# Four modulation sums moved to the first query stage, and wider rows of gates in DRAM

## The chip, the cores and the metric

The kernel runs on one core of one Trainium2 chip. The metric is device time in microseconds (us). Lower is better. Everything is computed in float32. Where the text says "parts", a float32 number has been cut into a high and a low part whose products are added up.

## The reference, cut to what matters

Two transformer blocks follow one another. The second block has two layers, and each layer ends in a PEER feed-forward: every token picks 16 of 16384 experts for each of 8 heads, and sums the experts' outputs by gate weights. Each layer has six modulation vectors, which are products of a condition with a 1024 x 6144 matrix.

```python
for i in range(DEPTH_2):                      # two layers, 0 and 1
    mod_x = jnp.split((silu_c @ ada_w[i] + ada_b[i])[:, None, :], 6, axis=-1)
    mod_c = jnp.split(silu_cc @ ada_w[i] + ada_b[i], 6, axis=-1)
    hx = modulate_2(x, norm_mix[i], mod_x[0], mod_x[1])
    hc = modulate_2(ctx, norm_mix[i], mod_c[0], mod_c[1])
    ...                                       # attention of layer i
    x = x + mod_x[2] * yx
    hx = modulate_2(x, norm_ffn[i], mod_x[3], mod_x[4])
    if last:
        x = x + mod_x[5] * peer(hx, peer_w_q[i], peer_keys[i], peer_u[i], peer_v[i])
    else:
        ...                                   # the 256 context tokens too
        y = peer(jnp.concatenate([hc, hx], axis=1), peer_w_q[i], ...)

def peer(h, w_q, sub_keys, u_tab, v_tab):
    q = (t @ w_q).reshape(b * n, PEER_HEADS, 2, PEER_KEY_DIM)
    s = jnp.einsum('thcd,hcnd->thcn', q, sub_keys)      # then top-k: expert, gate
    act = jax.nn.gelu(jnp.einsum('td,thkd->thk', tb, jnp.take(u_tab, eb, axis=0)))
    return jnp.einsum('thk,thkd->td', gb * act, jnp.take(v_tab, eb, axis=0))
```

## The kernel before

**Stages and queues.** The kernel is a list of stages. Each engine runs the stages in order, by its own program. A stage's first instruction on an engine waits (`enter`) until the stage before it has raised `stage_done`. SyncE (SP) issues, in one order written out by hand, the loads of the weights into a ring of four slots of 1 MB (`ring<-in_weights`, line 3576), and among them the other loads and stores of the PEER stages. ScalarE (ACT) and GpSimd (POOL) issue DMAs of their own.

**The PEER feed-forward of layer index 0** works on 512 tokens. Its stages are these:

- `Norm`.
- `PeerQuery` makes the queries: 8 chunks of weights, each cut into parts by ACT (L280) and VectorE (DVE, L286), with 48 matmuls of 512 columns per chunk on TensorE (PE; L319 for the first two chunks, L2310 for the other six). At its start ACT stores the 2 MB of `xT` in DRAM (`x_kept<-xT`, L2322).
- `PeerScores`.
- `PeerHidden` walks over 64 pairs of expert rows. 384 tokens are done densely, as if each token used all experts. The other 128 tokens ("gathered") fetch their own rows by indirect DMA (L2500, dot products L2534). From pair 33 on it also makes the dense matrix of gates, eight tokens (a "lot") at a time, two lots for a pair: DVE makes one-hot rows (L3054 to L3059), PE multiplies them (L2955), and ACT copies the result into one of two blocks in SBUF (L2864). A block holds 32 tokens, so four lots. It is stored to DRAM in four pieces of 512 KB (`gates<-arena`, L2776), one after each of the next lots, and ACT may write over a block only when its pieces of two blocks before have landed. Activations are also stored, for each pair (L2759).
- `PeerValues` walks over the 64 pairs again. SP loads gates (L3210) and activations (L3214), DVE multiplies them (L3293) and makes low parts (L3297, L3300), ACT makes high parts (L3271), and PE does 48 matmuls of 384 columns per pair (L3377). Beside this POOL gathers the rows of values (L3115) for the 128 other tokens into five buffers, and DVE adds them (L3132), two for a pair. `first_loads` fetches the first two groups of gates near the end of `PeerHidden`.

Layer index 1 has the same stages for 256 tokens.

**Side modulation.** The modulation vectors are not made on PE. POOL loads tiles of 512 KB of the modulation matrix (`arena<-in_side_weights`, L557) into four buffers in turn, each when the step that read the buffer before is done. DVE multiplies each tile by a column of the condition and adds it to a running sum: 8 tiles to a sum, the first by L574, the others by L577. This is done in groups, beside a stage that has room. Before, the fourth and last group (`SECOND`) makes all of layer index 1's vectors beside `PeerValues` of layer index 0: eight sums (vectors 0 and 1 under two conditions, 2 to 5 under one), 48 tiles and 64 steps, one step for each pair. PE later turns the sums into columns (`SideTurn`): vectors 0 and 1 in the `Norm` that follows, vectors 2 to 5 (`second_rest`) after the attention of layer index 1.

**The gates in DRAM** are laid out per partition as (group of expert rows, block of 32 tokens, rows of the group x 32 tokens). A group has 4 rows, so the run that one block writes is 4 x 32 x 4 bytes = 512 bytes. A load of a group's gates is one piece of 12 x 512 bytes for each partition.

The lines that set the layout and the order of loads are these:

```python
GATE_ROWS = (4, 4)
...
sp.dma_start(self.gates[:, groups, b, :],
             self.block[:, b % 2, rows, :].rearrange("column (group row) t -> column group (row t)", row=each))
...
def vector(self, dve):                       # PeerQuery
    self.k.enter(dve, self.s)
    each_chunk(dve, 8, lambda c, r, i: self.w.low(dve, c, r))
```

In `PeerQuery` the low parts of chunks 0 and 1 are made ahead, in the `Norm` before it, and `low` skips them. There are two buffers for parts, so chunk 2's high part is made when PE has finished chunk 0.

Of the kernel before, what the change touches and what calls it, by code (L numbers as in the profile page):

```python
# [8 lines left out]
F32 = mybir.dt.float32  # L9
# [38 lines left out]
GATE_BLOCK = (32, 32)  # L48
GATE_ROWS = (4, 4)

# [53 lines left out]
class Signal:  # L104


    def __init__(self, sem, base):
        self.sem, self.base = sem, base
# [17 lines left out]
class Core:  # L126


    def __init__(self, nc, ctx, io):
# [375 lines left out]
class SideModulation:  # L505


    FIRST_BLOCK, MLA_FIRST, MLA_LATER, SECOND = range(4)

    def __init__(self, k):  # L510
# [4 lines left out]
        own = [k.hT[:, 4 * i:4 * i + 4, 0:SEQ] for i in range(2)]  # L515
        self.buffers = [wide(22528, 4), wide(22528, 4), wide(4096, 2) + wide(14336, 2), wide(19456, 4)]
        self.sums = [wide(26624, 4) + context + [lru], context + wide(26624, 4),
                     wide(24576, 6), own + context[1:] + wide(25600, 5)]
# [6 lines left out]
        self.steps = k.count_of("side_steps", sum(DT * len(c) for g in self.groups for _, _, c in g))  # L525
        self.work, self.totals = [], []
        n_tiles, n_steps = 0, 0
        for g, group in enumerate(self.groups):
            work, totals = [], []
            for layer, m, conds in group:  # L530
                mine = list(range(len(totals), len(totals) + len(conds)))
                totals += [[layer, m, cond, 0] for cond in conds]
                for t in range(DT):
                    ops = []
                    for total, cond in zip(mine, conds):
                        n_steps += 1
                        ops.append((total, cond, t, totals[total][3], n_steps))
                        totals[total][3] = n_steps
                    work.append((n_tiles, ops))
                    n_tiles += 1  # L540
            self.work.append(work)
            self.totals.append(totals)
# [7 lines left out]
    def loads(self, pool, g):  # L550


        buffers = self.buffers[g]
        for i, (n, _) in enumerate(self.work[g]):
            if i >= 4:
                pool.wait_ge(self.steps.sem, self.steps.at(self.work[g][i - 4][1][-1][4]))
            pool.dma_start(self.like(buffers[i % 4], buffers[i % 4]), self.k.io["side_weights"][n])\  # L557
                .then_inc(self.loaded[i % 4].sem, 16)
            yield

    def like(self, flat, other):
        return flat if len(other.shape) == 2 else flat.rearrange("p (a b) -> p a b", b=SEQ)

    def begin(self, dve, g):

        def steps():
            for i, (n, ops) in enumerate(self.work[g]):
                w = self.buffers[g][i % 4]
# [11 lines left out]

        self.todo, self.total = steps(), sum(len(ops) for _, ops in self.work[g])
        self.done = 0
# [29 lines left out]
class SideTurn:  # L612
# [10 lines left out]
    def tensor(self, pe):  # L623
        side, k = self.side, self.side.k
        for n, i in enumerate(self.which):
            pe.wait_ge(side.steps.sem, side.steps.at(side.totals[self.g][i][3]))
            total = side.sums[self.g][i]
            for q in range(DT):
# [1015 lines left out]
class TokenProduct(Stage):  # L1644
# [6 lines left out]

    def __init__(self, k, name, n_k, tiles, lhs, out, at=None, norm=None, steps={}, norm_rows={}, chain=None):
        self.norm, self.steps, self.norm_rows = norm, steps, norm_rows
        self.chain = chain or (norm and norm.chain)
# [5 lines left out]
        self.act_copied = k.count_of("rows_act_copied", self.even[-1])  # L1660
        self.dve_copied = k.count_of("rows_dve_copied", self.odd[-1])

    def wait_bank(self, pe):
# [587 lines left out]
def diff_stages(k, normed, second_rest):  # L2251
# [13 lines left out]
                            10: ([("roots", 1)], [("scale", 1)]), 11: ([], [("rotate", 1)])},  # L2265
                     norm_rows={0: 1, 1: 3}),
    ]
# [18 lines left out]
class PeerQuery(Stage):  # L2286

    def __init__(self, k, l, T, h, queries):  # L2290
        self.k, self.s, self.T, self.h, self.q = k, k.stage(), T, h, queries
# [42 lines left out]
    def vector(self, dve):  # L2334
        self.k.enter(dve, self.s)
        each_chunk(dve, 8, lambda c, r, i: self.w.low(dve, c, r))
        self.finish(dve, (self.copied, 8), *([(self.kept, 16)] if self.kept else []))


class PeerScores(Stage):  # L2340

    def __init__(self, k, l, n, high, queries, scores):
        self.k, self.s, self.g, self.n, self.q, self.scores = k, k.stage(), FIRST[f"peer{l}_keys"], n, queries, scores
        self.products = k.count_of("peer_scores", n)
        self.copied = k.count_of("peer_scores_copied", n)
# [835 lines left out]
class PeerValues(PeerTable):  # L3183
# [61 lines left out]
    def sync(self, sp, load):  # L3245
# [13 lines left out]

        walk(sp, 0, self.pairs, 4, body)  # L3260

# [66 lines left out]
    def gpsimd(self, pool):  # L3328
# [4 lines left out]
        if self.side:  # L3333
            work, loads = self.side.work[self.side.SECOND], self.side.loads(pool, self.side.SECOND)
            ends = np.cumsum([len(ops) for _, ops in work]).tolist()
            issued = 0
# [107 lines left out]
def peer_stages(k, l, side=None, gate=None):  # L3444
# [6 lines left out]
    scores = k.room(work, T // P, 2 * PEER_HEADS, P)  # L3451
    before = [Norm(k, [p[:4] for p in parts], high, after=gate), PeerQuery(k, l, T, (high, k.hT_split[:, :, 0:T]), queries),
              PeerScores(k, l, T // P, high, queries, scores)]
    hidden = PeerHidden(k, l, T - (SPREAD if l else GATHERED), scores, work)
# [38 lines left out]
def program(nc, io):  # L3493

    with ExitStack() as ctx:
# [20 lines left out]
        peer_gate = turn(2, (5,), 7)  # L3516
        second_gain = turn(3, (0, 1), 1, layer=(1, 0))
        second_rest = turn(3, (2, 3, 4, 5), 7, layer=(1, 1), column=SEQ)
        lru = Recurrence(k)
# [224 lines left out]
```

## Time and profile before

| | us |
|---|---|
| median of three runs | 3320.55 |
| lowest, highest | 3320.46, 3329.16 |
| the profiled execution, its own time | 3321.39 |
| its span, first to last instruction | 3319.5 |
| around the span | 1.89 |
| TensorE's mean granted clock | 0.983 |

Times in the profile count from the start of the span. Engine "busy" is time in instructions, "PEclk" is the clock that TensorE was granted (1.00 is 2.4 GHz, 0.50 is 1.2 GHz), and the DMA share is the mean busy share of the core's 16 DMA engines. For layer index 0, `PeerQuery` runs from 1033 to 1124 us, `PeerHidden` from 1141 to 1741, and `PeerValues` from 1741.6 to 2274.4. The part of `PeerHidden` in which gates are made is about 1420 to 1676.

### The profile page before, as it was taken

What the parts mean: (1) busy time and instruction counts of PE and PEld (TensorE: products, weight loads), DVE (VectorE), ACT (ScalarE), POOL (GpSimd) and SP (SyncE); (2) the same over time, 40 slices, a digit from 0 to 9 for tenths busy, and PEclk for the clock granted to TensorE, in tenths of its full rate; (3) what the DMA queues carried; (4) which work ended last, traced back from release to release, by engine and by line L of the source; (5) the groups of instructions that cost most, each with busy time, mean ns of one, the idle gap of its engine ahead of it and who ended that gap; (6) DMA issues with size and microseconds to landing.
All of it is one profiled execution on the core that took longest, in us unless ns stands there. A gap on an engine that the chain in (4) does not pass through costs nothing.

```text
span 3319.5 us, 52879 instructions
## 1 busy us (share of the span) xinstructions
PE 3176.7 (96%) x20142; PEld 2920.0 (88%) x20142; DVE 2481.6 (75%) x4079; ACT 1466.8 (44%) x1864; POOL 1063.9 (32%) x706
## 2 busy tenths in 40 slices
PE   7999889999999999999999999999988999999999
PEld 5998689856777899999999999998868898989998
DVE  6877568686764479878849999897665797757777
ACT  5434444322443333366633333334234567874443
POOL 0110000010000278877763335551000698721110
PEclk9999899999999999999999999999998999999999
DMA  8984157461012267799999999994203578999996
GB/s 321 333 307 171 47 190 251 160 228 61 4 39 102 94 228 273 267 323 384 380 393 393 379 377 411 409 409 175 93 1 120 183 237 300 386 370 333 351 350 231
DMA packets 305610, 835.27 MB, mean 252 GB/s; under 512 B 22432, under 2 KB 185504, under 8 KB 254368
## 3 DMA queue, kind: packets, MB, share of 16 engines
q1 hardware_dynamic: 180096, 534.82, 44.3%
q0 software_dynamic: 67968, 247.49, 19.3%
q10 hardware_dynamic: 57376, 50.72, 4.5%
q8 instruction: 104, 1.70, 0.2%
q14 instruction: 66, 0.54, 0.0%
HBM read 750.10 MB, written 82.84 MB: 251 GB/s over the span
## 4 chain that ended last, share of the span: by engine, by line
PE 82%; DVE 5%; DMA 5%; ACT 3%; POOL 2%; issue 1%; SPq 1%; another core or an unknown queue 0%; ACTq 0%; DVEq 0%; POOLq 0%
PE ps L3377 16%; PE ps L2936 11%; PE ps L862 7%; PE ps L3360 6%; PE ps L2912 5%; PE ps L1688 5%; PE ps L873 4%; PE ps L3362 3%; PE ps L2310 3%; DMA gates<-arena 3%; PE ps L2914 3%; PE ps L319 3%; PE ps L1430 2%; PE ps L1412 2%; POOL arena_split L2886 2%; PE ps L2150 2%
## 5 line engine op out<-in xcount | busy, mean ns | idle before, releaser
L2886 POOL TENSOR_TENSOR arena_split<-ring,arena_split 128x1024 fp32r<-128x1024 f32 x228 | 570.9, 2515 | 900.6 <-ACT arena_split L2804 898.3
L2936 PE MATMUL ps<-xT_split,arena_split 128*128 128x384 f32 x2048 | 534.0, 337 | 3.1 <-ACT xT L2834 2.6
L3377 PE MATMUL ps<-arena_split 128*128 128x384 f32 x3072 | 532.7, 334 | 2.3 <-DVE arena_split L3300 2.3
L3377 PEld LDWEIGHTS ps<-arena_split 128*128 128x128 f32 x3072 | 532.5, 188 | 2.6 <-issue 2.6
L286 DVE TENSOR_TENSOR arena_split<-ring,arena_split 128x2048 fp32r<-128x2048 f32 x128 | 292.9, 2291 | 245.1 <-ACT arena_split L280 244.3
L3271 ACT ACTIVATE arena_split<-ring 128x2048 fp32r<-128x2048 f32 x126 | 241.7, 1918 | 492.1 <-PE ps L3377 306.6
L280 ACT ACTIVATE arena_split<-ring 128x2048 fp32r<-128x2048 f32 x128 | 244.4, 1915 | 376.9 <-PE ps L862 133.3
L2936 PEld LDWEIGHTS ps<-xT_split,arena_split 128*128 128x128 f32 x2048 | 371.8, 188 | 4.2 <-issue 4.2
L3297 DVE TENSOR_TENSOR arena_split<-ring,arena_split 128x2048 fp32r<-128x2048 f32 x128 | 293.2, 2291 | 94.8 <-ACT arena_split L3271 86.6
L2912 PE MATMUL ps<-hT_split,arena_split 128*128 128x448 f32 x1024 | 338.7, 379 | 6.9 <-POOL arena_split L2886 3.9
L557 POOL DMA_DIRECT2D arena<-in_side_weights x152 | 82.8, 546 | 817.5 <-DVE arena L577 285.0
L2936 PE MATMUL ps<-hT_split,arena_split 128*128 128x384 f32 x1024 | 342.9, 335 | 0.0
L3360 PE MATMUL ps<-arena_split 128*128 128x448 f32 x1024 | 327.2, 379 | 0.8 <-DVE arena_split L3300 0.8
L2914 PE MATMUL ps<-hT_split,arena_split 128*128 128x224 f32 x1024 | 273.7, 267 | 0.0
L2804 ACT ACTIVATE arena_split<-ring 128x1024 fp32r<-128x1024 f32 x256 | 268.9, 1053 | 8.4 <-DMA ring<-in_weights 8.4
L3362 PE MATMUL ps<-arena_split 128*128 128x224 f32 x1024 | 271.0, 265 | 0.0
L3115 POOL DMA_INDIRECT arena<-in_weights,arena x128 | 214.9, 1679 | 137.7 <-DVE hT L3132 116.3
L862 PE MATMUL ps<-arena_split 128*128 128x256 f32 x1280 | 230.9, 283 | 3.2 <-DVE arena_split L286 3.2
L2912 PEld LDWEIGHTS ps<-hT_split,arena_split 128*128 128x128 f32 x1024 | 194.5, 190 | 23.0 <-issue 7.9
L3360 PEld LDWEIGHTS ps<-arena_split 128*128 128x128 f32 x1024 | 191.9, 187 | 21.0 <-DVE arena_split L3297 1.0
L862 PEld LDWEIGHTS ps<-arena_split 128*128 128x128 f32 x1280 | 199.8, 192 | 3.6 <-DVE arena_split L286 3.6
L2914 PEld LDWEIGHTS ps<-hT_split,arena_split 128*128 128x128 f32 x1024 | 197.6, 193 | 0.0
(355 smaller groups left out, 6339.9 us busy)
## 6 DMA issues: line engine op xcount, KB each, us to landing
ring<-in_weights SPq DMA_DIRECT2D x396, 1024.0 KB
arena<-in_side_weights POOLq DMA_DIRECT2D x152, 512.0 KB, 5.6
gates<-arena SPq DMA_DIRECT2D x76, 512.0 KB
arena<-gates SPq DMA_DIRECT2D x32, 768.0 KB
arena<-activations SPq DMA_DIRECT2D x64, 384.0 KB
activations<-xT ACTq DMA_DIRECT2D x128, 112.0 KB
arena<-gates SPq DMA_DIRECT2D x32, 448.0 KB
arena<-activations SPq DMA_DIRECT2D x64, 224.0 KB
```

What stands on the lines that cost most here:

```text
L280: act.activation(self.w[:, r % self.bufs, 0, :], self.k.ring[:, chunk % RING, :], ACT.Copy).then_inc(self.highs.sem, 1)
L286: dve.tensor_tensor(self.w[:, r % self.bufs, 1, :], self.k.ring[:, (self.g + r) % RING, :], self.w[:, r % self.bufs, 0, :].bitcast(F32), A ...
L862: mm = pe.matmul(k.ps[:, self.BANKS[r % 4], j * SEQ:(j + 1) * SEQ], w.tile(r, a, j * DT + t), self.h[b][:, t, :], start=n == 0, stop=n == ...
L2804: act.activation(self.u[:, 2 * (f % 2) + j, 0, :], self.raw(f)[:, j, :], ACT.Copy).then_inc(self.u_high.sem, 1)
L2886: pool.tensor_tensor(low, self.raw(f)[:, j, :], high.bitcast(F32), ALU.subtract)\
L2912: pe.matmul(both, self.u[:, u, 0, t * P:(t + 1) * P], self.h_both[:, t], start=t == 0, stop=True, skip_group_check=True)
L2914: mm = pe.matmul(both[:, 1, :], self.u[:, u, 1, t * P:(t + 1) * P], self.h_both[:, t, 1, :], start=False, stop=True, skip_group_check=True)
L2936: mm = pe.matmul(k.ps[:, j, 0:self.T], self.u[:, 2 * (f % 2) + j, a, t * P:(t + 1) * P], self.h[b][:, t, :], start=n == 0, stop=n == 3 * D ...
L3297: dve.tensor_tensor(self.v[:, par, 1, :], k.ring[:, (self.g + f) % RING, :], self.v[:, par, 0, :].bitcast(F32), ALU.subtract).then_inc(k.c ...
L3360: pe.matmul(both, self.v[:, f % 2, 0, at], self.weighted[:, f % 2, :, j, :], start=first(c, 1) and j == 0, stop=True, skip_group_check=True)
L3362: mm = pe.matmul(both[:, 1, :], self.v[:, f % 2, 1, at], self.weighted[:, f % 2, 0, j, :], start=False, stop=True, skip_group_check=True)
L3377: mm = pe.matmul(k.ps[:, t, self.from_token:self.from_token + self.T], self.v[:, f % 2, a, j * D + t * P:j * D + (t + 1) * P], self.weight ...
```

## The change

It does three things.

1. The sums of vectors 2 to 5 of layer index 1 (32 tiles, 32 steps) leave the group beside `PeerValues` and become a group of their own, `REST`, beside `PeerQuery` of layer index 0: after each of the 8 chunks' low parts DVE takes four steps. POOL loads their tiles there, stores each finished sum to DRAM (512 KB each, `park`), and loads the four sums back (`reload`) at the start of the `diff_qkv` stage of layer index 1. ACT in `PeerScores` waits for the first sum's store, because the scores are written over its place.
2. A group of gates for layer index 0 has 8 rows in place of 4. The run in DRAM is 1 KB, a group's load is 1.5 MB in place of 768 KB, and there are 16 of them in place of 32. SP's loop over pairs in `PeerValues` takes 8 pairs at a time, and a group is loaded four pairs ahead of its first use or more.
3. The rows of values go through six buffers in place of five, at other places.

```diff
-GATE_ROWS = (4, 4)
+GATE_ROWS = (8, 4)
...
+        self.side_dram = nc.dram_tensor("side_kept", [P, 4, D], F32).ap()
...
-                       [(1, m, (1, 2) if m < 2 else (1,)) for m in range(6)]]
+                       [(1, m, (1,)) for m in range(2, 6)],
+                       [(1, m, (1, 2)) for m in range(2)]]
...
+    def park(self, pool):
+
+        for i, total in enumerate(self.totals[self.REST]):
+            pool.wait_ge(self.steps.sem, self.steps.at(total[3]))
+            pool.dma_start(self.k.side_dram[:, i, :], self.sums[self.REST][i]).then_inc(self.parked[i > 0].sem, 16)
+
+    def wait_parked(self, eng):
+
+        for signal, n in zip(self.parked, (1, 3)):
+            eng.wait_ge(signal.sem, signal.at(16 * n))
+
+    def reload(self, pool):
+
+        for i, room in enumerate(self.back):
+            pool.dma_start(room, self.k.side_dram[:, i, :]).then_inc(self.reloaded.sem, 16)
...
     def tensor(self, pe):                       # SideTurn
         side, k = self.side, self.side.k
+        if self.g == side.REST:
+            pe.wait_ge(side.reloaded.sem, side.reloaded.at(16 * 4))
...
     def vector(self, dve):                      # PeerQuery
         self.k.enter(dve, self.s)
-        each_chunk(dve, 8, lambda c, r, i: self.w.low(dve, c, r))
+        if self.side:
+            self.side.begin(dve, self.side.REST)
+            for c in range(8):
+                self.w.low(dve, c, c)
+                self.side.run(self.side.total * (c + 1) // 8)
+        else:
+            each_chunk(dve, 8, lambda c, r, i: self.w.low(dve, c, r))
         self.finish(dve, (self.copied, 8), *([(self.kept, 16)] if self.kept else []))
 
+    def gpsimd(self, pool):
+        if self.side:
+            self.k.enter(pool, self.s)
+            self.side.load(pool, self.side.REST)
+            self.side.park(pool)
+            self.side.wait_parked(pool)
...
+        if self.side:                           # PeerScores, ACT
+            act.wait_ge(self.side.parked[0].sem, self.side.parked[0].at(16))
...
-        rooms = [15872 + D * i for i in range(3)] + [23552, 24576]
+        rooms = [23552, 24576] + [26624 + D * i for i in range(4)]
...
-        walk(sp, 0, self.pairs, 4, body)        # PeerValues, SP
+        walk(sp, 0, self.pairs, 2 * pairs_of, body)
```

## Rows read from the trace of the kernel before

**Rows 1.** The page: busy time, share of the span, instructions, of each engine

```profile
PE 3176.7 (96%) x20142; PEld 2920.0 (88%) x20142; DVE 2481.6 (75%) x4079; ACT 1466.8 (44%) x1864; POOL 1063.9 (32%) x706
```

**Rows 2.** Windows: start:end, length, busy of each engine, PEclk, DMA share, GB/s

```profile
1420.00:1676.00 256.00, 249.60 (x1921) 240.12 (x1919) 209.78 (x344) 164.55 (x145) 186.39 (x123) 1.00 1.03 369
1676.00:1741.60 65.60, 60.68 (x342) 59.79 (x340) 23.79 (x35) 22.13 (x29) 46.72 (x34) 0.97 1.04 393
1741.60:2274.40 532.80, 532.78 (x3074) 532.77 (x3075) 483.62 (x383) 170.10 (x127) 234.15 (x167) 1.00 0.99 389
```

**Rows 3.** Chain of work that ended last: start, us, what

```profile
1057.53 65.29 PE ps L2310 x288
...
1479.37 12.47 DMA gates<-arena
```

**Rows 4.** Waits of PE and of ACT between 1420 and 1760: total, times, longest

```profile
PE ps L2955 <- ACT arena L2864: 5.8, 10, 1.1
...
ACT arena L2864 <- DMA gates<-arena: 20.6, 10, 2.6
```

**Rows 5.** Timelines of DVE and ACT's queue at the start of PeerQuery

```profile
1043.92 0.07 DVE L649 MEMSET small<- 128x8 f32 x1
1054.26 2.29 DVE L286 TENSOR_TENSOR arena_split<-ring,arena_split 128x2048 fp32r<-128x2048 f32 x1 [10.28 <-ACT arena_split L280]
...
1043.73 0.35 ACTq L2322 DMA_DIRECT2D x_kept<-xT  x1
```

**Rows 6.** Another group's first loads and steps, timelines of DVE and POOL, from 667 us

```profile
671.65 1.42 DVE L574 TENSOR_SCALAR arena<-arena,cs 128x1024 f32<-128x1024 f32 x2 [4.90 <-DMA arena<-in_side_weights]
672.98 16.82 DVE L577 SCALAR_TENSOR_TENSOR arena<-arena,cs 128x1024 f32<-128x1024 f32 x14
...
667.71 2.08 POOL L557 DMA_DIRECT2D arena<-in_side_weights  x4 [50.22 <-ACT hT L705]
```

**Rows 7.** Side tiles: landing over the whole run, and between 1745 and 2000

```profile
DMA to landing us min/median/max: 3.5/5.6/12.1
...
arena<-in_side_weights POOLq DMA_DIRECT2D x16, 512.0 KB, 9.1
```

**Rows 8.** Windows about PeerQuery and the norm before it (columns as in rows 2)

```profile
1029.00:1033.40 4.40, 0.00 (x0) 0.00 (x0) 4.37 (x8) 1.70 (x4) 0.00 (x0) 0.72 0.00 0
1033.40:1035.40 2.00, 1.94 (x5) 1.55 (x6) 2.00 (x7) 0.91 (x2) 0.00 (x0) 0.50 0.00 0
1035.40:1037.40 2.00, 2.00 (x6) 1.58 (x5) 2.00 (x6) 1.30 (x3) 0.00 (x0) 0.50 0.00 0
...
1044.00:1048.00 4.00, 4.00 (x19) 3.34 (x18) 0.00 (x0) 0.00 (x0) 0.00 (x0) 1.00 0.93 393
...
1058.00:1124.00 66.00, 64.81 (x286) 53.32 (x285) 11.52 (x6) 15.84 (x12) 0.00 (x0) 1.00 0.26 95
```

**Rows 9.** DMA queues between 1484 and 1652: packets, MB, share of 16 engines

```profile
q1 hardware_dynamic: 35584, 33.41, 57.2%
```

**Rows 10.** The same between 1745 and 2000

```profile
q1 hardware_dynamic: 15056, 56.50, 58.6%
```

**Rows 11.** End of PeerHidden: timelines of SP's and ACT's queue, and windows

```profile
1709.71 0.27 SPq L3210 DMA_DIRECT2D arena<-gates  x1
...
1719.46 0.49 ACT L2834 ACTIVATE xT<-ps 128x384 f32<-128x384 f32 x1 [8.31 <-DMA activations<-xT]
...
1704.00:1708.00 4.00, 4.00 (x25) 4.00 (x24) 1.41 (x4) 3.08 (x5) 3.72 (x2) 1.00 1.03 430
...
1716.00:1720.00 4.00, 1.99 (x12) 1.67 (x10) 1.23 (x2) 0.54 (x2) 2.34 (x2) 1.00 1.00 409
1720.00:1724.00 4.00, 3.91 (x14) 3.94 (x15) 1.77 (x3) 0.89 (x1) 2.37 (x1) 0.57 1.05 419
```

**Rows 12.** DVE's last steps in PeerValues, and window of the diff_qkv stage

```profile
2265.30 5.44 DVE L3132 SCALAR_TENSOR_TENSOR hT<-arena,hT 128x1024 f32<-128x1024 f32 x4
...
2310.00:2410.00 100.00, 98.25 (x433) 81.08 (x434) 62.86 (x53) 27.05 (x22) 0.00 (x0) 1.00 0.30 106
```

More of the change, by code:

```diff
@@ L505 @@
 class SideModulation:
-    FIRST_BLOCK, MLA_FIRST, MLA_LATER, SECOND = range(4)
+    FIRST_BLOCK, MLA_FIRST, MLA_LATER, REST, SECOND = range(5)
     def __init__(self, k):
@@ L538, in __init__ @@
                         totals[total][3] = n_steps
-                    work.append((n_tiles, ops))
+                    tile = {None: m - 2, 0: 7 + m, 1: 13 + m}[layer] * DT + t
+                    work.append((n_tiles, tile, ops))
                     n_tiles += 1
@@ L553, in loads @@
         buffers = self.buffers[g]
-        for i, (n, _) in enumerate(self.work[g]):
+        for i, (_, tile, _) in enumerate(self.work[g]):
             if i >= 4:
-                pool.wait_ge(self.steps.sem, self.steps.at(self.work[g][i - 4][1][-1][4]))
-            pool.dma_start(self.like(buffers[i % 4], buffers[i % 4]), self.k.io["side_weights"][n])\
+                pool.wait_ge(self.steps.sem, self.steps.at(self.work[g][i - 4][2][-1][4]))
+            pool.dma_start(self.like(buffers[i % 4], buffers[i % 4]), self.k.io["side_weights"][tile])\
                 .then_inc(self.loaded[i % 4].sem, 16)
             yield
+    def park(self, pool):
[8 more added lines that the diff above has]
+            pool.dma_start(room, self.k.side_dram[:, i, :]).then_inc(self.reloaded.sem, 16)
     def like(self, flat, other):
@@ L566, in steps @@
         def steps():
-            for i, (n, ops) in enumerate(self.work[g]):
+            for i, (n, _, ops) in enumerate(self.work[g]):
                 w = self.buffers[g][i % 4]
@@ L579, in steps @@
                     yield
-        self.todo, self.total = steps(), sum(len(ops) for _, ops in self.work[g])
+        self.todo, self.total = steps(), sum(len(ops) for _, _, ops in self.work[g])
         self.done = 0
@@ L624, in tensor @@
         side, k = self.side, self.side.k
+        if self.g == side.REST:
+            pe.wait_ge(side.reloaded.sem, side.reloaded.at(16 * 4))
         for n, i in enumerate(self.which):
             pe.wait_ge(side.steps.sem, side.steps.at(side.totals[self.g][i][3]))
-            total = side.sums[self.g][i]
+            total = side.back[i] if self.g == side.REST else side.sums[self.g][i]
             for q in range(DT):
@@ L1644, with __init__ @@
 class TokenProduct(Stage):
-    def __init__(self, k, name, n_k, tiles, lhs, out, at=None, norm=None, steps={}, norm_rows={}, chain=None):
-        self.norm, self.steps, self.norm_rows = norm, steps, norm_rows
+    def __init__(self, k, name, n_k, tiles, lhs, out, at=None, norm=None, steps={}, norm_rows={}, chain=None,
+                 reload=None):
+        self.norm, self.steps, self.norm_rows, self.reload = norm, steps, norm_rows, reload
         self.chain = chain or (norm and norm.chain)
@@ L2265, in diff_stages @@
                             10: ([("roots", 1)], [("scale", 1)]), 11: ([], [("rotate", 1)])},
-                     norm_rows={0: 1, 1: 3}),
+                     norm_rows={0: 1, 1: 3}, reload=second_rest.side.reload),
     ]
@@ L2286, with __init__ @@
 class PeerQuery(Stage):
-    def __init__(self, k, l, T, h, queries):
-        self.k, self.s, self.T, self.h, self.q = k, k.stage(), T, h, queries
+    def __init__(self, k, l, T, h, queries, side=None):
+        self.k, self.s, self.T, self.h, self.q, self.side = k, k.stage(), T, h, queries, side
         self.w = SplitWeights(k, FIRST[f"peer{l}_q"], 8, 16384)
@@ L3334, in gpsimd @@
             work, loads = self.side.work[self.side.SECOND], self.side.loads(pool, self.side.SECOND)
-            ends = np.cumsum([len(ops) for _, ops in work]).tolist()
+            ends = np.cumsum([len(ops) for _, _, ops in work]).tolist()
             issued = 0
@@ L3451, in peer_stages @@
     scores = k.room(work, T // P, 2 * PEER_HEADS, P)
-    before = [Norm(k, [p[:4] for p in parts], high, after=gate), PeerQuery(k, l, T, (high, k.hT_split[:, :, 0:T]), queries),
-              PeerScores(k, l, T // P, high, queries, scores)]
+    before = [Norm(k, [p[:4] for p in parts], high, after=gate), PeerQuery(k, l, T, (high, k.hT_split[:, :, 0:T]), queries, side),
+              PeerScores(k, l, T // P, high, queries, scores, side)]
     hidden = PeerHidden(k, l, T - (SPREAD if l else GATHERED), scores, work)
@@ L3516, in program @@
         peer_gate = turn(2, (5,), 7)
[L3517 to L3518 removed]
+        second_gain = turn(side.SECOND, (0, 1), 1, layer=(1, 0))
+        second_rest = turn(side.REST, (2, 3, 4, 5), 7, layer=(1, 1), column=SEQ)
         lru = Recurrence(k)
```

15 lines of the change are left out of this document (12 added, 3 removed).

## The prediction, made before the changed kernel was run

> **What bounds the kernel now.** I read the page's busy times first. The reader is to see that PE is busy for 96% of the span [rows 1], so the kernel can lose some 140 us of idle PE at most, and only in the stages that the change touches. Next I cut those stages into windows [rows 2]. The values stage, from which the four sums are taken, has PE busy 532.78 of 532.80 us, although the DMA engines are full too (0.99, 389 GB/s) and DVE has 484 us of work. Nothing taken from DVE or DMA there shortens it. The stretch in which gates are made has PE idle for 256.0 - 249.6 = 6.4 us, and the rest of the hidden stage for 65.6 - 60.7 = 4.9 us. Then the chain of waits, which runs through stores of gates [rows 3], and the list of waits, which shows how little that is: PE waited 5.8 us, in ten short stops, for ACT's copy of a lot, and ACT for the stores of gates 20.6 us [rows 4]. So the most that wider rows can give is known before any price: 6.4 us there, and beside it what the junction holds. Last I read the start of the query stage by timeline, because that is where work is added.
>
> **Queries: 32 steps and 32 loads added.** Six chunks take PE 65.29 us, 10.9 us each, and PE reaches chunk 2 at 1057.5 [rows 3]. The stage opens at about 1044.0, when DVE is done with the norm and ACT has issued the 2 MB store of x [rows 5]. DVE now idles 10.3 us until it makes chunk 2's low part, 1054.26 to 1056.55, which is 1.0 us before PE wants it. In the new order the steps for chunks 0 and 1, eight of them, stand ahead of that low part on DVE, and each waits for a tile of its own. POOL can issue the loads only from 1044.0. So what was idle time becomes a wait for DMA, and behind it are chunk 2's low part and PE.
>
> The lower bound: in another group the first step began 3.9 us after the first load was issued (671.65 - 667.71), and steps ran without a gap, the first of a sum 0.7 us and each other 16.82 / 14 = 1.2 us [rows 6]. If this holds here, the steps run from 1047.9 to 1057.0, the low part ends 2.3 us later at 1059.3, and PE is 1.8 us late. The likely value goes by bytes, because here a tile is used by one step and there by two: the store of x (2.1 MB) and eight tiles (4.2 MB) have to pass. The store alone ran at 393 GB/s [rows 8], so 6.3 MB take 16.0 us, until 1060.0. One step (1.3) and the low part (2.3) follow: 1063.6, PE 6.1 us late. At the 345 GB/s that I take for mixed traffic at worst (an estimate, an eighth below those 393) it is 8.4 us. I take 6.1, since the rows' own rate is the nearest.
>
> After idle PE runs at the half clock for a while: the 4.4 us of idle in the norm were followed by 4 us at 0.50, which is 2.0 us of lost work [rows 8]; 2.0 us of idle before 1720 by 4 us at 0.57, 1.7 us lost [rows 11]. So add 2.0. The term is +8.1, with bounds of +1.8 and +10.4.
>
> The later chunks stay covered. Per chunk DVE has 2.3 + 4 x 1.2 = 7.1 us against PE's 10.9, and DMA has 2.1 MB more on top of 95 GB/s, 290 GB/s in all, below 393. If a tile took over (10.9 - 2.3) / 4 = 2.15 us, this cover would go too (a rival below). The last steps end some 5 us after chunk 7's low part, which is made while PE has chunks 6 and 7 (22 us) before it. POOL then parks four sums, and its next work is in the hidden stage, 25 us later. ACT's new wait in the scores is for a sum complete after eight steps, 60 us before. Reloading 2.1 MB in the diff_qkv stage costs 5 us of DMA time where the DMA share is 0.30 [rows 12], and PE wants it only after the attention. All of these I cost at nothing. Without the cover, the park would cost at most its landing, 12.1 us by the slowest tile [rows 7].
>
> **Values: 32 steps and 16.8 MB removed.** DVE loses 41 us and DMA 8% of its 207 MB. PE covers both, so the gain is nothing. At the end of the stage one step and the row additions still stand in the last pair; they ended at 2270.7, 3.6 us before PE [rows 12, 2]. The sixth buffer speeds up gathers for which DVE does not idle. A group of gates is now wanted four pairs (33 us) after its load is issued, so its double size is covered.
>
> **Gates in runs of 1 KB.** Between 1484 and 1652 SP's queue moved 2048 packets of the ring (8 KB) and some 33,500 short ones, mostly runs of 512 bytes, in 57.2% of 16 engines' 168 us, 1538 engine-us [rows 9]. In the values stage the same queue, with mostly long packets, moved 56.5 MB in 58.6% of 4080 engine-us, 23.6 bytes per ns [rows 10]. At that price the ring took 711 us, so a short packet took (1538 - 711) / 33,500 = 24.7 ns against 21.7 by its bytes: 3.0 ns over. If long packets go at the fastest window's 430 GB/s, 26.9 bytes per ns [rows 11], the same sum gives 27.3 ns against 19.0: 8.3 over. Half of 32,768 gate packets less, divided by 16 engines, saves 3.1 to 8.5 us in 168, or 4.7 to 13 us of DMA time in the 256 us, against 6.4 us of idle PE. So DMA gets nearly out of PE's way, and I take -5.4; the bounds are 0, if the pieces land as late as before, and -6.4. The Trainium skill ("DMA: Bandwidth & Descriptors", Specifications) has 512 bytes as the smallest transfer for full line rate; by that rule 512-byte runs are as good as longer ones and this term is 0. The rows speak against it, by the 3 ns that a short packet costs over its bytes.
>
> **The junction.** `first_loads` now brings two groups of 1.5 MB in place of 768 KB, 1.6 MB more, 4.0 us at 393 GB/s, from 1709.71 on, just where ACT waited for its own stores (8.31 us before 1719.46) and PE for ACT [rows 11]. Against it there are five pieces of gates with half the packets and a shorter backlog. The bounds are +4.0 and -(4.9 + 1.7) = -6.6, all idle and slow clock gone. The two pull opposite ways, and I take 0.
>
> **The sum** against the profiled execution's own time: 3321.4 + 8.1 - 5.4 + 0 = 3324.1. The median of before is 0.8 below that execution, so 3323.3.
>
> **Rivals.** A measurement of this kernel can tell about 0.3%, 10 us, from no change.
>
> - *The side tiles fit.* If the tiles come as fast as in rows 6, the queries lose 1.8 us, and with all idle PE of the gates and junction gone: 3320.6 + 1.8 - 6.4 - 6.6 = 3309.4; with half of the junction's, 3312.7. For it: there are four loads in flight at once. Against it: the store of x stands in front. Chance 0.20, of which 0.06 beyond -0.3%.
> - *The other side: side tiles come slower than DVE wants them, in every chunk.* With four buffers, a landing of L gives one tile every L / 4. In the full DMA of the values stage L is 9.1 us [rows 7], 2.3 us a tile: the eighth tile lands 9.1 + 7 x 2.3 = 25.2 us after 1044.0, PE is 25.2 + 3.6 - 13.5 = 15.3 us late, five more chunks take 2.3 + 9.1 = 11.4 in place of 10.9 (+2.5), and 2.0 for the clock: +19.8, hence 3335.0. It decides (net over 10 us) from 2.0 us a tile, L = 8. Against it: here the median of all is 5.6. Chance 0.12.
> - *Wider runs save nothing*: the gate pieces land as late as before, and ACT waits the same 20.6 us for them. 3320.6 + 8.1 = 3328.7. The packet sums above speak against it, the unknown rate of long packets for it. Chance 0.13. This is also what the Trainium skill's 512-byte rule, cited above, would make of the change.
> - *The doubled first groups lengthen the junction*: 3323.3 + 4.0 = 3327.3. It needs the loads to be in the way of ACT's stores for their whole length. Chance 0.12.
> - *My forecast*, 3323.3, with its own range of 3318 to 3328. Chance 0.43.
>
> **How the numbers follow.** All cases but two lie within 3310.6 to 3330.5. Beyond the upper end is the slow-tile case with 0.10 of its 0.12, and 0.03 of the two before the last when their bounds add up. Faster 0.06, same 0.81, slower 0.13. The range of 3312 to 3333 leaves out less than 2 in 10: the best part of the first rival and most of the second.
>
> **What would show it.** Right: DVE's steps wait for `in_side_weights` after 1044, PE stops once for 4 to 8 us at the start of chunk 2 and is then granted 0.50 for about 4 us; the query stage lasts some 8 us longer; PE's ten waits for ACT's copy shrink to under 2 us in total; the values stage stays at 532.8 us. Wrong: no stop at chunk 2, stops at later chunks, gate stores that still release ACT, or a values stage of another length.

## The result: 1.0028 of the time before

| | us |
|---|---|
| before, median of 20 runs | 3321.41 |
| changed, median of 20 runs (lowest, highest) | 3332.2 (3327.58, 3337.81) |
| ratio, 95% interval | 1.0028 (1.0021 to 1.0036) |
| changed, the profiled execution, and its span | 3330.86, 3329.1 |

The kernel became some 9 us slower by the ratio; the two medians lie 10.8 us apart. I had forecast 3 us, no change that could be told. The figure lies in the range of 3312 to 3333, but only 0.8 us from its end, beyond my forecast's own 3318 to 3328, and at the edge of what I had called "same" (0.28% against 0.3%). One mechanism, forecast and priced too low, costs 12 us, more than the whole loss. The two other parts work against each other: the wider rows give about 5 us in the stretch of gates, and the junction, which I had put at nothing, takes 1 to 3 of them back.

In the changed kernel's program the lines have moved: L286 is L287 (low parts), L574 and L577 are L597 and L600 (side steps), L557 is L564 (side loads), L2776 is L2823 (stores of gates), L2310 is L2341 (queries), L2955 is L3002 and L2864 is L2911 (gates), L2936 is L2983, L3377 is L3424 (values).

First the chain of waits of the changed kernel, as start, us, what. It answers to [rows 3].

```profile
1042.66 9.39 DMA arena<-in_side_weights
1052.08 1.29 DVE arena L600
...
1056.44 5.49 DMA arena<-in_side_weights
1061.95 1.28 DVE arena L600
1063.23 2.21 DVE arena_split L287
1065.49 68.36 PE ps L2341 x288
...
1543.98 20.46 DMA gates<-arena
...
1752.07 532.75 PE ps L3424 x3072
```

The reader is to see that side tiles, side steps and chunk 2's low part now stand in the chain ahead of PE's six chunks, and that these take 68.4 us in place of 65.3. The values stage is as long as before. Then PE's waits between 1025 and 1160 (total, times, longest):

```profile
PE ps L2341 <- DVE arena_split L287: 9.1, 1, 9.1
```

Windows of the query stage from the end of chunk 1 on (columns as in [rows 2]):

```profile
1056.30:1065.40 9.10, 0.04 (x1) 0.00 (x0) 7.25 (x6) 2.82 (x2) 2.63 (x5) 0.77 0.77 265
1065.40:1067.40 2.00, 1.91 (x5) 1.53 (x6) 1.90 (x3) 0.00 (x0) 0.53 (x1) 0.50 0.97 297
1067.40:1069.40 2.00, 2.00 (x6) 1.60 (x5) 1.79 (x3) 0.00 (x0) 0.76 (x2) 0.50 1.04 418
1069.40:1073.00 3.60, 3.60 (x13) 2.82 (x12) 3.37 (x3) 0.00 (x0) 0.82 (x2) 0.72 1.01 415
...
1056.30:1134.00 77.70, 68.38 (x289) 56.01 (x288) 47.45 (x34) 15.31 (x12) 15.30 (x29) 0.93 0.76 287
```

PE stops once, for 9.1 us, and then loses 2.0 us at 0.50 and 1.0 us at 0.72: 12.1 us in all, which is just the 77.7 us against 65.6 from 1057.4 to 1123.0 in the kernel before. DVE's timeline shows what it waited for:

```profile
1050.90 0.75 DVE L597 TENSOR_SCALAR arena<-arena,cs 128x1024 f32<-128x1024 f32 x1 [8.77 <-DMA arena<-in_side_weights]
1052.08 5.45 DVE L600 SCALAR_TENSOR_TENSOR arena<-arena,cs 128x1024 f32<-128x1024 f32 x4 [0.42 <-DMA arena<-in_side_weights]
1057.84 1.28 DVE L600 SCALAR_TENSOR_TENSOR arena<-arena,cs 128x1024 f32<-128x1024 f32 x1 [0.31 <-DMA arena<-in_side_weights]
1060.15 1.28 DVE L600 SCALAR_TENSOR_TENSOR arena<-arena,cs 128x1024 f32<-128x1024 f32 x1 [1.02 <-DMA arena<-in_side_weights]
1061.95 1.28 DVE L600 SCALAR_TENSOR_TENSOR arena<-arena,cs 128x1024 f32<-128x1024 f32 x1 [0.51 <-DMA arena<-in_side_weights]
1063.15 2.28 DVE L287 TENSOR_TENSOR arena_split<-ring,arena_split 128x2048 fp32r<-128x2048 f32 x1
```

The first tile comes 8.8 us after the first load is issued (1042.14), and the last three of the eight come one by one, each some 2 us after the one before.

**Lengths by stage.** One trace is not enough for the rest, since a single execution varies by some us. The table takes the traces of all runs below. "Gates" is the stretch from 274.6 us after the hidden stage's first matmul to the last one-hot matmul (to 0.5 us), "junction" from there to the values stage, "values" from its first matmul to its last one's start.

| run | rows, first groups | gates | junction | values |
|---|---|---|---|---|
| before | 4, both ahead | 257.3 | 65.0 | 532.4 |
| e8, before again | 4, both ahead | 260.2 | 64.0 | 534.0 |
| e2 | 4, both ahead | 255.7 | 63.0 | 532.4 |
| e3 | 4, both ahead | 254.9 | 64.5 | 532.4 |
| changed | 8, both ahead | 254.2 | 66.0 | 532.4 |
| e1 | 8, both ahead | 251.3 | 66.0 | 533.9 |
| e4 | 8, both ahead | 250.8 | 70.5 | 534.2 |
| e5 | 8, second later | 252.7 | 59.5 | 533.3 |
| e6 | 8, second later | 252.5 | 60.0 | 533.6 |
| e11, e6 again | 8, second later | 251.5 | 59.5 | 533.3 |
| e9 | 4, second later | 256.2 | 63.0 | 532.4 |
| e10 | 4, second later | 256.3 | 63.0 | 532.4 |
| e7 | 2, both ahead | 292.5 | 68.0 | 534.5 |

The last column varies as well. In e1, e4 and e8 PE was busy all through it, but it began at the low clock, behind PE's stop in the junction: the granted clock was 0.75 and 0.50 in the first 4 us of e1 and 0.50 in those of e4. So 1.5 to 2 us of those rows belong to the junction. In e5, e6 and e11 it holds 0.6 to 0.9 us of idle PE.

### The profile page after: what moved, and what is told of

Same layout as the page of the kernel before. It is cut to its first block, busy times and chain, and to the rows that moved or that the text cites. A ratio compares the mean times of both kernels' runs of the same rounds, so it can differ in the third digit from the quotient of the medians.

```text
span 3329.1 us, 52776 instructions
## 1 busy us (share of the span) xinstructions
PE 3181.7 (96%) x20142; PEld 2923.7 (88%) x20142; DVE 2486.7 (75%) x4079; ACT 1463.5 (44%) x1864; POOL 1032.3 (31%) x714
## 4 chain that ended last, share of the span: by engine, by line
PE 85%; DVE 6%; DMA 4%; ACT 3%; POOL 1%; issue 1%; SPq 1%; ACTq 0%; DVEq 0%; POOLq 0%
PE ps L3424 16%; PE ps L2983 14%; PE ps L887 7%; PE ps L3407 6%; PE ps L1719 5%; PE ps L2959 5%; PE ps L898 4%; PE ps L2341 3%; PE ps L3409 3%; PE ps L2961 2%; PE ps L1455 2%; PE ps L1437 2%; PE ps L3002 2%; PE ps L320 2%; PE ps L2181 1%; PE ps L1003 1%
## 5 line engine op out<-in xcount | busy, mean ns | idle before, releaser
L2983 PE MATMUL ps<-xT_split,arena_split 128*128 128x384 f32 x2048 | 534.5, 337 | 4.1 <-ACT xT L2881 4.1
L3424 PE MATMUL ps<-arena_split 128*128 128x384 f32 x3072 | 532.8, 334 | 2.0 <-DVE arena_split L3347 2.0
L3424 PEld LDWEIGHTS ps<-arena_split 128*128 128x128 f32 x3072 | 532.5, 188 | 2.3 <-issue 2.3
L287 DVE TENSOR_TENSOR arena_split<-ring,arena_split 128x2048 fp32r<-128x2048 f32 x128 | 292.9, 2292 | 207.9 <-ACT arena_split L281 207.0
L564 POOL DMA_DIRECT2D arena<-in_side_weights x152 | 81.6, 538 | 1102.7 <-DVE hT_split L766 319.7
L2983 PEld LDWEIGHTS ps<-xT_split,arena_split 128*128 128x128 f32 x2048 | 372.6, 189 | 4.7 <-issue 4.7
L2983 PE MATMUL ps<-hT_split,arena_split 128*128 128x384 f32 x1024 | 343.3, 335 | 0.0
L3162 POOL DMA_INDIRECT arena<-in_weights,arena x128 | 182.5, 1426 | 267.0 <-DVE hT L3179 240.2
L2959 PEld LDWEIGHTS ps<-hT_split,arena_split 128*128 128x128 f32 x1024 | 194.3, 190 | 23.0 <-issue 7.8
L2581 DVE SCALAR_TENSOR_TENSOR arena<-arena,ps 128x1024 f32<-128x1024 f32 x128 | 153.8, 1217 | 62.0 <-DMA arena<-in_u_rows,arena 60.9
```

What stands on the lines that cost most here:

```text
L287: dve.tensor_tensor(self.w[:, r % self.bufs, 1, :], self.k.ring[:, (self.g + r) % RING, :], self.w[:, r % self.bufs, 0, :].bitcast(F32), A ...
L2959: pe.matmul(both, self.u[:, u, 0, t * P:(t + 1) * P], self.h_both[:, t], start=t == 0, stop=True, skip_group_check=True)
L2983: mm = pe.matmul(k.ps[:, j, 0:self.T], self.u[:, 2 * (f % 2) + j, a, t * P:(t + 1) * P], self.h[b][:, t, :], start=n == 0, stop=n == 3 * D ...
L3424: mm = pe.matmul(k.ps[:, t, self.from_token:self.from_token + self.T], self.v[:, f % 2, a, j * D + t * P:j * D + (t + 1) * P], self.weight ...
```

## The experiments

The theory was that DVE waits for side tiles ahead of chunk 2's low part, that wider runs take DMA out of PE's way, and that the junction is even. The rivals were side tiles too slow in every chunk, runs whose length does not matter, and a junction made longer by the doubled first groups.

**e1: the steps behind chunk 2's low part.**

```diff
-                self.side.run(self.side.total * (c + 1) // 8)
+                self.side.run(self.side.total * max(0, c - 1) // 6)
```

> The changed kernel with its 32 side steps taken after the low parts of chunks 2 to 7 only (5, 5, 6, 5, 5, 6 of them), none ahead of chunk 2's. Theory (DVE waits for tiles ahead of chunk 2's low part, PE waits for DVE): PE's 9.1 us stop at the start of chunk 2 and the 3 us of slow clock behind it go, the query stage falls from 77.7 us back to about 65.6 from chunk 2 on, and the whole to about 12 us below the changed kernel, that is 1 to 4 us below the kernel before. Rival (side tiles are too slow in every chunk): the stop moves to chunk 3 or 4, because 5 to 6 tiles a chunk want 1.6 us a tile, and most of the 12 us stay.

Measured: 1.0000 of the kernel before (0.9991 to 1.0008), 3323.35 us. Between 1025 and 1160 PE's waits hold

```profile
PE ps L2341 <- DVE arena_split L287: 2.5, 3, 1.0
```

So the 9.1 us stop is gone, and with it the slow clock behind it. What stays are three stops of at most 1 us. PE's six chunks take 68.8 us (1057.0 to 1125.8), against 65.4 by the same count before (1057.4 to 1122.8). The loss is gone, but the 1 to 4 us below the kernel before that I expected did not come: the rival has a small part, because five or six tiles a chunk come too slowly.

**e2, e3: groups of 4 rows**, in the changed kernel and in e1's.

```diff
-GATE_ROWS = (8, 4)
+GATE_ROWS = (4, 4)
...
-        walk(sp, 0, self.pairs, 2 * pairs_of, body)
+        walk(sp, 0, self.pairs, 4, body)
```

> The changed kernel with groups of 4 rows (512-byte runs) as before, all else as changed. Theory (wider runs free DMA time): the stretch of gates goes back from 253.5 to about 256.5 us and PE's waits for ACT's copy from 2.5 to about 6 us, the junction loses its 0.9 us; 2 us slower than the changed kernel, 1.0035 of the kernel before. Rival (run length gives nothing, the shorter stretch was chance): the stretch stays at 253 to 254 us.

> The changed kernel with both: steps late and groups of 4 rows. What is left of the change is 32 steps moved out of the values stage, the park and the reload, and six buffers. Theory (PE covers the values stage and all of these): the same as before within 2 us, values stage 532.8. Rival (moving DMA out of the values stage helps, or park and reload cost something): more than 3 us off the kernel before, with the values or the diff_qkv stage of another length.

Measured: e2 1.0032 (1.0020 to 1.0045), e3 1.0005 (0.9995 to 1.0015). The stretch of gates is 255.7 and 254.9 us, above all runs with 8 rows, and PE's waits for ACT's copy are back at 5.2 and 4.8 us (changed kernel 2.5, e1 1.0). But the junction, which I had expected to give 0.9 us, falls to 63.0 and 64.5. The sum of both is 318.7 and 319.4 against 317.3 to 321.3 with 8 rows and both groups ahead. The medians say the same: e2 is 1.7 us above the changed kernel and e3 1.0 above e1, and the intervals overlap. So the wide rows as the change has them are worth next to nothing, though the parts of this zero are not zero. In e3 all else of the change is left (32 steps fewer beside the values, park, reload, six buffers). Its chunks still take 67.9 us, 2.5 too long, and the whole is 1.7 us above the kernel before by the medians, so the rest costs and gives nothing that these runs can tell.

**e4: the store of x later.**

```diff
-        if self.l == 0:
-            act.dma_start(k.x_dram, k.xT[:]).then_inc(self.kept.sem, 16)
...
             w.wait_used(act, c)
+            if self.l == 0 and c == 3:
+                act.dma_start(k.x_dram, k.xT[:]).then_inc(self.kept.sem, 16)
```

> The changed kernel with the 2 MB store of x issued by ACT at chunk 3 in place of the start of the stage; the steps stay where the change put them. Theory (the first tiles share DMA with the store of x): the first step begins about 4 us after the first load is issued in place of 8.8, the eighth ends near 1055 plus 1 to 2, and PE's stop at chunk 2 falls from 9.1 us to 2 to 4 us; 6 to 8 us faster than the changed kernel. Rival (the tiles are late for their own sake: POOL's issue, landing and four buffers): the stop stays at 7 us or more.

Measured: 1.0024 (1.0014 to 1.0033). PE's stop is 5.6 us, between my two expectations of 2 to 4 and 7 or more. The whole is 2.5 us below the changed kernel by the medians, not 6 to 8: the stop and its slow clock are some 4 us shorter, and in the profiled execution the junction is 4.5 us longer (70.5). DVE's timeline of e4:

```profile
1048.29 0.75 DVE L597 TENSOR_SCALAR arena<-arena,cs 128x1024 f32<-128x1024 f32 x1 [3.95 <-DMA arena<-in_side_weights]
...
1055.65 1.28 DVE L600 SCALAR_TENSOR_TENSOR arena<-arena,cs 128x1024 f32<-128x1024 f32 x1 [0.45 <-DMA arena<-in_side_weights]
1057.97 1.28 DVE L600 SCALAR_TENSOR_TENSOR arena<-arena,cs 128x1024 f32<-128x1024 f32 x1 [1.04 <-DMA arena<-in_side_weights]
1059.94 1.28 DVE L600 SCALAR_TENSOR_TENSOR arena<-arena,cs 128x1024 f32<-128x1024 f32 x1 [0.69 <-DMA arena<-in_side_weights]
```

And POOL's, which issues the loads:

```profile
1051.01 0.53 POOL L564 DMA_DIRECT2D arena<-in_side_weights  x1 [1.14 <-DVE arena L600]
1052.72 0.53 POOL L564 DMA_DIRECT2D arena<-in_side_weights  x1 [1.18 <-DVE arena L600]
1054.11 0.53 POOL L564 DMA_DIRECT2D arena<-in_side_weights  x1 [0.86 <-DVE arena L600]
```

The first tile lands after 3.9 us, as in [rows 6], so the store was in its way. The sixth to eighth are issued at 1051.01, 1052.72 and 1054.11, each only when a buffer is free, and used at 1055.65, 1057.97 and 1059.94: 4.6 to 5.8 us from issue to use. With the step (1.3) and POOL's issue (0.5) a buffer's round is about 7 us, a quarter of which is 1.8 us a tile. The DMA engines were not full meanwhile:

```profile
1054.00:1058.00 4.00, 3.86 (x18) 2.86 (x16) 2.52 (x3) 1.39 (x3) 1.05 (x2) 1.00 0.79 264
1058.00:1062.00 4.00, 0.00 (x0) 0.00 (x0) 3.31 (x3) 2.81 (x2) 1.54 (x3) 1.00 0.65 238
```

Of the 9.1 us, the store has 3.5, and the other 5.6 go with the buffers' round and DVE's place in the order. A run with more buffers, which would part these two, was not made.

**e5: the second group of gates later.** It is e1's kernel with this:

```diff
         for c in range(2):
-            self.gate_load(sp, c, c)
+            if c == 0 or self.l:
+                self.gate_load(sp, c, c)
             self.pair_loads(sp, c, c)
...
                 self.pair_loads(sp, c + 2, f)
+            if isinstance(c, int) and c == 1 and not self.l:
+                self.gate_load(sp, 1, 1)
```

> The kernel of e1 (steps late, 8 rows) with the second group of gates (1.5 MB) loaded at pair 1 of the values stage in place of the end of the hidden stage; it is first used at pair 4. Theory (the doubled first groups take back at the junction what the wider runs give in the stretch of gates: in four runs 8 rows had 252.0 and 67.3 us there, 4 rows 255.9 and 64.0): the junction falls from 66 to 70 us to 63 to 65, the stretch of gates stays at 251 to 254, the values stage at 532.8; about 3 us below e1. Rival (the junction's spread of 63 to 70 is chance, or set by the ring loads and the activations): it stays at 66 or more.

Measured: 0.9980 (0.9971 to 0.9989), 3317.21 us, with a junction of 59.5 us. That is more than I expected (63 to 65): 1.6 MB less ahead of the last stores of activations make the junction 6.5 us shorter than in e1, the kernel that differs only in this, and the ratios of the two (0.9980 and 1.0000) say the same. By bytes it would be 4 us. Windows of the stretch of gates and the junction, in the changed kernel and then in e5:

```profile
1432.10:1686.10 254.00, 251.31 (x1937) 242.97 (x1935) 209.69 (x344) 165.47 (x146) 186.77 (x124) 0.99 1.01 374
1686.10:1752.10 66.00, 59.95 (x335) 59.08 (x333) 23.78 (x35) 21.27 (x29) 47.37 (x34) 0.97 1.04 411
```

```profile
1425.70:1678.40 252.70, 249.42 (x1936) 241.26 (x1935) 209.69 (x344) 165.51 (x145) 187.00 (x124) 1.00 1.01 375
1678.40:1737.90 59.50, 58.34 (x335) 57.73 (x334) 23.70 (x35) 21.45 (x28) 43.71 (x31) 1.00 1.04 408
```

PE's idle time in the junction falls from 6.1 to 1.2 us, and the clock stays at 1.00. The rest is slow clock in the first.

**e6 and e11: four or five steps a chunk and ten behind the last**, on top of e5; the same kernel twice.

```diff
-                self.side.run(self.side.total * max(0, c - 1) // 6)
+                self.side.run((0, 0, 4, 8, 12, 17, 22, 32)[c])
```

> The kernel of e5 with the steps of the query stage spread 4, 4, 4, 5, 5, 10 behind the low parts of chunks 2 to 7 in place of 5, 5, 6, 5, 5, 6. Theory (a tile comes every 1.6 to 1.9 us there, so more than four steps make a chunk's low part late; e1 still lost 2.5 us of PE in three stops, and its chunks 2 to 7 took 68.4 us against 65.3): the stops go, the chunks take 65.3 to 66 us, 2 to 3 us below e5, about 0.998 of the kernel before. Rival (the ten steps behind the last chunk take 19 us, longer than PE's 21 us leave): the stage ends late by up to 3 us and nothing is gained.

> The kernel of e6 unchanged, beside e9 on one chip, for the difference of the two: 0.9974 of the kernel before within 0.001; stretch of gates 251 to 254, junction 59 to 61.

Measured: 0.9974 (0.9962 to 0.9987) and 0.9971 (0.9960 to 0.9982), 3314.1 and 3313.73 us. This is faster than both kernels, 8 us below the one before, and 3.1 us below e5, as expected. PE has no stop in the chunks, as the window of e6 over them shows, with DMA at 330 GB/s beside it:

```profile
1056.40:1121.70 65.30, 65.30 (x289) 53.76 (x287) 47.81 (x36) 15.17 (x11) 16.34 (x31) 1.00 0.92 330
```

**e7: groups of 2 rows in the kernel before.**

```diff
-GATE_ROWS = (4, 4)
+GATE_ROWS = (2, 4)
```

> The kernel before with groups of 2 rows for layer index 0: runs of 256 bytes in DRAM, 2048 of them in a piece, and nothing else changed. Theory (a short run costs its bytes and some ns on top): SP's queue moves twice the gate packets, at 13 to 18 ns each; the stretch of gates grows by 3 to 12 us. A threshold at 512 bytes (by a rule of the Trainium skill, DMA: Bandwidth & Descriptors, Specifications) would show as a jump: 256-byte runs much dearer than by half of the bytes, 25 ns or more each and the stretch 25 us longer or more, while 512 to 1024 bytes changed little.

Measured: 3365.7 us in one run, 43 us slower (44 between the two profiled executions). Of this, 35 us are in the stretch of gates (292.5 us), where PE now waits for ACT's copy 32.8 us in place of 5.8, and 3 in the junction (68.0), although the first two groups are half as large. The other 6 lie ahead of these stages and in the values, where e8 differs from the first trace by 3.0 and 1.6 us without any change. I had expected 3 to 12 us by a price per run, and 25 us or more by a threshold at 512 bytes. The second is what came, though the price of a run, below, is nearer to the first's 13 to 18 ns than to 25. PE's wait:

```profile
PE ps L2955 <- ACT arena L2864: 32.8, 5, 7.6
```

SP's queue in 168 us of that stretch, for runs of 256 bytes (e7) and then of 1 KB (the changed kernel):

```profile
q1 hardware_dynamic: 55884, 27.47, 59.1%
```

```profile
q1 hardware_dynamic: 19001, 33.34, 53.8%
```

By the prediction's way of counting (347 ns for a ring packet, 13 x 128 of them and 16 x 128) a short packet takes (1589 - 577) / 54,220 = 18.7 ns at 256 bytes and (1446 - 711) / 16,953 = 43.4 ns at 1 KB, beside the 24.7 ns at 512. For 512 bytes of gates that is 37.4, 24.7 and 21.7 ns. These are estimates, since the ring packet's 347 ns come from another stage. At the prediction's other price for it (305 ns, by 26.9 bytes per ns) the steps between the three are 12.6 and 3.0 ns in place of 12.7 and 3.0. Over the 49,152 runs of 512 bytes and 16 engines the steps are worth 39 us and 9 us of DMA time. The Trainium skill ("DMA: Bandwidth & Descriptors", Specifications) gives 512 bytes as the least for full rate. This trace agrees that the large step lies below 512 bytes, and it differs above: 3 ns are left there. Where DMA is full and PE waits for it, that is 4.8 us of this kernel by the means of the table.

**e8: the kernel before again.**

> The kernel before, unchanged, for a second trace of it: how far the stretch of gates (257.1 us in the first trace), the junction (65.0), the granted clock between scores and hidden stage and the start of the query stage vary by themselves. Theory: stretch within 254 to 258, junction within 63 to 66, sum of both within 3 us of the first. Rival (chance): the sum differs by more than the 3 to 4 us that I ascribe to the length of the runs.

Measured: one run, 3329.62 us, within the spread of the kernel before (to 3332.17). Its stretch of gates was 260.2 us, so outside the 254 to 258 that I expected, and its junction 64.0. Its transposes ahead of the hidden stage ran at the low clock, by themselves, as those of the changed kernel did. The chain of e8:

```profile
1142.55 5.38 PE ps L2476 x32
```

It took 3.84 us in the first trace of the same kernel, and 5.46 us in the changed one. So 1.6 us of the difference between the two traces is not of the change. e6 and e11, one kernel too, took 5.37 and 3.84 us.

**e9: e6 with groups of 4 rows; e10: the kernel before with the second group later.** The edits are those of e2 and of e5, with the second group loaded at pair 0, since it is used at pair 2.

> The kernel of e6 with groups of 4 rows; the second group, first used at pair 2 now, is loaded at pair 0. Theory (512-byte runs cost 4 to 5 us more in the stretch of gates, and with the second group out of the way nothing takes it back): stretch 255 to 258 in place of 252.5, junction 60 to 62 (768 KB less to load before it would be 2 us shorter, but more short packets behind it), so 3 to 5 us slower than e6, 0.9987 of the kernel before. Rival (wide runs give nothing beyond chance): within 1 us of e6.

> The kernel before with its second group of gates (768 KB) loaded at pair 0 of the values stage, nothing else. Theory (what is loaded ahead of the stage stands in the way of the last stores of activations): the junction falls from 64 to 65 us by about 2 us, the time of 768 KB at 400 GB/s; 0.9994 of the kernel before, within 0.3%. Rival (only the doubled group matters): no change of the junction.

Measured: e9 0.9997 (0.9988 to 1.0006), 3320.27 us beside 3313.73 of e11 on the same chip, so 6.5 us slower, more than the 3 to 5 that I expected, and the junction of 63.0 lies above my 60 to 62. The traces have 4.7 us of it in the stretch of gates and 3.5 in the junction, and 0.9 the other way in the values. Stretch of gates and junction of e9, then of e11:

```profile
1420.20:1676.40 256.20, 250.56 (x1938) 241.65 (x1937) 210.82 (x346) 164.76 (x146) 187.02 (x124) 1.00 1.03 371
1676.40:1739.40 63.00, 59.92 (x334) 59.03 (x333) 23.87 (x33) 21.17 (x28) 47.92 (x34) 0.97 1.03 392
```

```profile
1420.80:1672.30 251.50, 249.70 (x1938) 241.52 (x1937) 209.69 (x344) 165.80 (x146) 187.41 (x124) 1.00 1.01 378
1672.30:1731.80 59.50, 57.90 (x334) 57.61 (x333) 23.79 (x35) 20.74 (x27) 44.37 (x31) 1.00 1.04 404
```

The two differ in more than the runs' length: e9 has half of the bytes ahead of the junction (768 KB against 1.5 MB), and it is the longer one all the same.

e10 0.9999 (0.9990 to 1.0008), junction 63.0 against 64 and 65. That is 1 to 2 us, as expected, but e2 has 63.0 with both groups ahead, so it can't be told from chance. With groups of 768 KB there is little to gain by order; with 1.5 MB there is.

e9 and e10 together say what the moved sums are worth. e9 has them in the query stage, e10 has them beside the values, both have rows of 4 and the second group late, and both are as fast as the kernel before, within intervals of 3 us to either side. So the gain of e6 is all of the wide rows with the second group late, and none of the move. The move is needed all the same, for room in SBUF, which the code of the two kernels shows: the buffers of 8-row groups take 3072 columns (of float32, per partition) more than those of 4-row groups and reach over the places of three of the five row buffers (15872 to 18944), and the new places of the row buffers (26624 to 30720) are free in the values stage only because four sums have left them.

## Why the prediction was right, and where it was too low

The range held, by 0.8 us; the forecast in it did not. The two terms that missed, the stop and the junction, both erred to the same side, and one microsecond more would have carried the figure out of the range. That it held owes something to luck.

**The stop at chunk 2 (+8.1 forecast, 12.1 measured).** Right in mechanism, place and number of stops; e1 takes it away. The term was mis-sized: I let 6.3 MB pass at 393 GB/s, the rate of the store alone, and the eighth tile came 19.8 us after the first issue, 318 GB/s. Two things held it down. Store and tiles together did not reach 393 GB/s at first even with the engines full (0.99), as this window of the changed kernel shows:

```profile
1046.00:1050.00 4.00, 4.00 (x19) 3.34 (x18) 0.00 (x0) 0.00 (x0) 0.00 (x0) 1.00 0.99 318
```

Later four buffers whose loads wait for steps do not keep DMA full (e4's 0.79 and 0.65 above); e4 shows 5.6 of the 9.1 us without the store. My upper bound of 8.4 us was too low as well, since it was the same sum at a lower rate and had no term for the round. The clock took 3.0 in place of 2.0.

**The later chunks "covered".** Right for the changed kernel with four steps a chunk, but thin: with five or six, e1 lost 3 us. The rival of slow tiles rested on this cover. My sum for where it decides was off there: at 2.0 us a tile (L = 8) its own terms give 22.0 + 3.6 - 13.5 + 2.0 - 5.4 = +8.7 us net, so it takes some 2.1 us a tile to pass 10.

**The wide runs (-5.4 forecast).** Means of the table's stretches are 257.0 us for the four traces with 4 rows and both groups ahead, and 252.2 for the six with 8 rows, 4.8 less. The two sets do not overlap (254.9 to 260.2 and 250.8 to 254.2). PE's idle time there fell from 6.4 to 2.7 us in the changed kernel's trace. In the same trace the waits that I had named as signs are these:

```profile
PE ps L3002 <- ACT arena L2911: 2.5, 3, 2.1
ACT arena L2911 <- DMA gates<-arena: 15.2, 9, 3.8
```

PE's ten waits became three, 2.5 us in place of "under 2". One of my signs of being wrong came too, in part: gate stores still release ACT, for 15.2 us in place of 20.6 [rows 4].

**The junction (0 forecast).** This step failed. 8 rows with both groups ahead give 66.0, 66.0 and 70.5, mean 67.5, against 64.1: +3.4, or +1.9 without e4's 70.5, and +1.0 in the pair of traces of the two kernels. It is the rival with 12%, at or below its price of +4.0. I was right that two pulls oppose each other and wrong that they are equal. With the second group of 1.5 MB out of the way the junction is 59.5, 60.0 and 59.5 us, so having it ahead costs 6.5 us (e1 against e5), not 4.0. And with 1.5 MB ahead in both, 8 rows have these 59.7 us where 4 rows have 64.1, so the wide rows give 4.4.

**The values stage, park, reload, six buffers (0).** Right. DVE fell from 484 to 449 us (35 us, where I had said 41) and DMA from 0.99 to 0.92 in this window, and PE took 532.8 us:

```profile
1752.10:2284.90 532.80, 532.80 (x3075) 532.77 (x3076) 448.73 (x351) 166.95 (x127) 182.69 (x135) 1.00 0.92 355
```

The terms as measured are +12.1 - 4.8 + 3.4 = +10.7 us, against 9.3 by the ratio (0.0028 x 3321) and 10.8 by the medians. The two profiled executions taken alone differ by 9.6 us: -1.1 until PE reaches chunk 2, +12.1, +1.6 for the transposes' clock, -3.1 in the stretch of gates, +1.0 in the junction and -0.9 behind the values.

## What to carry to other kernels

When work is moved to a stage where an engine idles, ask what that idle time precedes. Here DVE's 10 us of idle lay just ahead of the one instruction that PE needed next. The same work behind that instruction cost 3 us with five or six steps a chunk, and nothing with four or five. A load that has slack is best kept out of the last microseconds before a stage change when DMA is full: 1.5 MB there cost 6.5 us, though for 768 KB no cost could be told from chance. And price the parts of a change apart. This one sums to a small loss and held a gain of 0.3%, all of it in one part (the wide rows, once their second group loads late); the moved sums gave no time, only the room for it.

## What the runs showed of the hardware

Runs of 256 bytes cost SP's queue some 18.7 ns, of 512 bytes 24.7 and of 1 KB 43.4 (estimates from its share and packets), beside saturated DMA engines. Halving the run from 512 bytes made the stretch of gates 35 us longer, doubling it made it 5 us shorter. Side tiles through four buffers came one in 1.8 us, 290 GB/s (an estimate from e4's round), while the DMA share was 0.79 and 0.65. Store and tiles together moved 318 GB/s at a share of 0.99, where the store alone had 393 at 0.93. The same 32 transposes, in executions of one kernel, took 3.84 or 5.38 us. Taking 1.6 MB out of the 60 us before a stage change shortened them by 6.5 us, more than the 4 us of its bytes; that the surplus is slow clock and queueing of ACT's stores behind SP's loads was not tried apart.
